# Two gated linear-attention mixers of a 1024-wide block: decay levels gathered into runs on four row groups, index scores side by side, gate by softplus, latent norms behind the products

## The reference, cut to what matters

```python
h = rmsnorm(x, g);  parts = split(h @ w_in)           # w_in: 1024 x 6744
o_mla  = causal attention; q = (rmsnorm(cq)*g) @ w_q_up, k,v = (rmsnorm(ckv)*g) @ w_kv_up
o_conv = cb * conv3(cc * cx)
rel = relu(iq . ik * 32**-0.5)                        # 8 index heads of 32
score = sum over heads of w * rel; top 64 keys of each token
o_dsa  = attention over the selected keys
a   = log_sigmoid(glr @ w_gate_up + b) / 16           # one number a key channel and token
cum = cumsum(a) inside chunks of 64 tokens
o_gla  = (q*exp(cum)) @ state  +  sum_j [q_i . (k_j * exp(cum_i - cum_j))] v_j   # j <= i in the chunk
state  = exp(last) * state + (k * exp(last - cum))^T v
merged = sum over the 4 branches of sigmoid(gate_n) * (o_n @ w_branch_n);  x = x + merged @ w_out
```

## Time and profile before

| what | value |
|---|---|
| median of 3 runs | 1791.27 us (1790.5 to 1792.84) |
| the profiled execution, its own time | 1794.49 us |
| its span in the trace | 1792.3 us |
| mean granted TensorE clock | 0.998 |
| busy: TensorE, VectorE, ScalarE, GpSimd | 99%, 71%, 53%, 2% of the span |
| HBM read | 306.57 MB, 172 GB/s over the span |
| first large mixer | about 936 to 1170 us |

### The profile page before, as it was taken

How to read it: one execution, slowest core, us unless ns; L and a number is a source line. 1 busy time by engine, 2 the same in 40 slices (tenths; PEclk the granted TensorE clock), 3 DMA queues, 4 the chain that set the end, 5 groups by cost and what they waited for, 6 DMA issues and landing times.

```text
span 1792.3 us, 24908 instructions
## 1 busy us (share of the span) xinstructions
PE 1775.2 (99%) x9702; PEld 1511.4 (84%) x9702; DVE 1271.8 (71%) x1933; ACT 948.2 (53%) x1346; POOL 30.2 (2%) x39
## 2 busy tenths in 40 slices
PE   9999999999999999999999999999999999999998
PEld 8888878888888888788888788888888878888887
DVE  7774795776577657777656977777756778677774
ACT  6554655555455546555545545455544644555553
POOL 0000000000000001000000000000000000000000
PEclk9999999999999999999999999999999999999999
DMA  8666523666566555366655534556655443456653
GB/s 272 191 179 201 176 71 96 197 183 194 175 200 184 194 176 182 107 198 189 193 183 180 179 118 130 180 182 188 190 191 171 141 156 129 152 184 194 190 195 108
DMA packets 227678, 309.25 MB, mean 173 GB/s; under 512 B 22558, under 2 KB 176318, under 8 KB 227562
## 3 DMA queue, kind: packets, MB, share of 16 engines
q1 hardware_dynamic: 227398, 307.35, 55.0%
q10 hardware_dynamic: 164, 0.30, 0.0%
HBM read 306.57 MB, written 1.05 MB: 172 GB/s over the span
## 4 chain that ended last, share of the span: by engine, by line
PE 90%; DVE 6%; ACT 2%; issue 1%; SPq 0%; DMA 0%; POOL 0%; POOLq 0%; ACTq 0%; DVEq 0%
PE ps L645 26%; PE ps L596 15%; PE ps L598 15%; PE ps L597 14%; PE ps L647 13%; DVE wlo L1733 2%; PE ps L1141 1%; PE ps L608 1%; PE ps L816 1%; DVE ev_acc L1742 1%; PE ps L842 1%; ACT whi L1239 1%; PE ps L829 1%; PE ps L784 0%; DVE m_scr L1742 0%
## 5 line engine op out<-in xcount | busy, mean ns | idle before, releaser
L1733 DVE TENSOR_TENSOR wlo<-staging,whi 128x1024 fp32r<-128x1024 f32 (+1 forms) x580 | 692.9, 1211 | 336.7 <-ACT whi L1239 336.3
L1239 ACT ACTIVATE whi<-staging 128x1024 fp32r<-128x1024 f32 (+1 forms) x580 | 606.3, 1050 | 476.9 <-PE ps L598 293.1
L645 PE MATMUL ps<-hT,whi 128*128 128x512 f32 x1984 | 624.0, 396 | 0.6 <-DVE wlo L1733 0.6
L647 PEld LDWEIGHTS ps<-hT,wlo 128*128 128x128 f32 x1984 | 372.7, 188 | 88.0
L647 PE MATMUL ps<-hT,wlo 128*128 128x256 f32 x1984 | 389.8, 278 | 0.0
L645 PEld LDWEIGHTS ps<-hT,whi 128*128 128x128 f32 x1984 | 302.0, 189 | 0.8 <-DVE wlo L1733 0.8
L596 PE MATMUL ps<-whi,fh 128*128 128x512 f32 x504 | 196.1, 389 | 0.0
L597 PE MATMUL ps<-wlo,fh 128*128 128x512 f32 x504 | 196.1, 389 | 0.0
L598 PE MATMUL ps<-whi,fl 128*128 128x512 f32 x504 | 196.1, 389 | 0.0
L596 PE MATMUL ps<-whi,hT 128*128 128x512 f32 (+3 forms) x464 | 184.7, 398 | 0.8 <-DVE wlo L1733 0.6
L598 PE MATMUL ps<-whi,hT 128*128 128x512 f32 (+3 forms) x464 | 177.4, 382 | 0.0
(11 more groups left out here) (349 smaller groups left out, 1913.2 us busy)
## 6 DMA issues: line engine op xcount, KB each, us to landing
staging<-in_w_in SPq DMA_DIRECT2D x92, 512.0 KB, 3.4
staging<-in_ffn_w_gate SPq DMA_DIRECT2D x84, 512.0 KB, 4.4
staging<-in_ffn_w_up SPq DMA_DIRECT2D x84, 512.0 KB, 4.5
staging<-in_ffn_w_down SPq DMA_DIRECT2D x84, 512.0 KB, 4.1
staging<-in_w_ffn_gate SPq DMA_DIRECT2D x44, 512.0 KB, 4.4
staging<-in_w_ffn_up SPq DMA_DIRECT2D x44, 512.0 KB, 4.6
staging<-in_w_ffn_down SPq DMA_DIRECT2D x44, 512.0 KB, 4.2
staging<-in_od_w_in SPq DMA_DIRECT2D x16, 512.0 KB, 4.3
```

The lines of the kernel that those rows point to most:

```text
L645: e.matmul(o, wh[:, kk, j * 128:j * 128 + 128], hT[:, k, :], start=k == 0, stop=False)
L647: m = e.matmul(o[:, 0:256], wl[:, kk, j * 128:j * 128 + 128], hTh[:, k, :], start=False, stop=k == KD - 1)
L1239: e.activation(high(u)[:, 0:n], stage[u % NS][:, 0:n], ACT.Copy).then_inc(*K.inc("hi", ("hi", u)))
L1733: e.tensor_tensor(low_of(u)[:, 0:n], stage[u % NS][:, 0:n], high(u)[:, 0:n].bitcast(F32), ALU.subtract).then_inc(*K.inc("lo", ("lo", u)))
```

## The change

1. *Levels.* Levels 0 to 3 run together, then 4 to 6. Each (level, head) is on its own row group of 32; the two chunks of a token tile are two column groups of 64, so only the diagonal 64x64 blocks are computed (masks 64 wide). A run takes four banks, one a head. Level runs are in rounds 25 and 30, `go` in 34, the GLA transposes in 42. Four pairs of buffers for scaled k and q instead of two.
2. *Selections* go into a buffer `near` (64 wide) by `gathered`, and ScalarE copies `near` into the padded `gat` in its round 32; its copy of `go` is in its round 33. VectorE's selections are in its rounds 25 (level 0), 27, 28, 29, 30 and 31 (levels 5 and 6).
3. *Index scores:* four row groups at a time, one group of 8 matmuls a token tile in place of two of 4.
4. *State products:* chunks 0, 1, 2 in one round, two banks, on alternating halves of the rows.
5. *Gate:* bias and log-sigmoid are one ScalarE `Softplus` with negated scale and bias; the factor -1/16 moves into the later exponentials. `glT` and `gup` have all 128 rows, the added ones zero (GpSimd memset, and SyncE waits for it before the parameter load).
6. *Latent norms:* VectorE no longer scales `nat` ahead of the `cq` transposes; the factor goes into the copies of `qn` (ScalarE) and `kn` (ScalarE, VectorE).
7. GpSimd clears `near` once; some VectorE steps of the GLA output are joined.

```diff
+    def take_two(self, one, two):
+        at = {b: n for n, b in enumerate(self.free)}
+        beside = [(b, b + 1) for b in at if b + 1 in at]
+        pair = min(beside, key=lambda p: max(at[p[0]], at[p[1]])) if beside else tuple(self.free[0:2])
...
 # TensorE, index scores
-                        for h0 in (0, 2):
-                            ps = room_pair((P, "idx", t, h0), (P, "idx", t, h0 + 1))
-                            for j in range(2):
-                                for x in range(2):
+                        ps = [b for h0 in (0, 2) for b in room_two((P, "idx", t, h0), (P, "idx", t, h0 + 1))]
+                        for j in range(2):
+                            for x in range(4):
...
 # TensorE, gla
-                    for c in range(3):
-                        t, p0 = c // 2, 64 * (c % 2)
-                        ps = room((P, "st", c))
-                        e.matmul(ps[:, 0:256], m.kd[p0:p0 + 64, t, :], N(936, 1192, t)[p0:p0 + 64, :], ...)
-                        yield
-                    for lev in range(7):
...
+                    ps = [room((P, "st", x)) for x in range(2)]
+                    for c in range(3):
+                        t, x = c // 2, c % 2
+                        w = e.matmul(ps[x][:, 256 * t:256 * t + 256], m.kd[64 * x:64 * x + 64, t, :],
+                                     N(936, 1192, t)[64 * x:64 * x + 64, :], start=True, stop=True)
...
+                    for some in (range(0, 4), range(4, 7)):
+                        for _ in range(7 if some[0] == 0 else 5):
+                            yield
+                        ps = [b for h in (0, 2) for b in room_two((P, "lev", some[0], h), (P, "lev", some[0], h + 1))]
+                        e.wait_ge(*K.at(P, "ql", some[-1]))
+                        for lev in some:
+                            kk, qq = (m.gk, m.gq) if lev == 0 else (m.kl[lev % 4], m.ql[lev % 4])
+                            for t in range(2):
+                                c = 128 * (lev % 4) + 64 * t
+                                for h in range(4):
+                                    for half in range(2):
+                                        sl = slice(t * 128 + 64 * half, t * 128 + 64 * half + 64)
+                                        w = e.matmul(ps[h][64 * half:64 * half + 64, c:c + 64],
+                                                     kk[32 * h:32 * h + 32, sl], qq[32 * h:32 * h + 32, sl], ...)
+                        for h in range(4):
+                            done(P, "lev", some[0], h)
+                    for _ in range(3):
+                        yield
+                    yield
                     for t in range(2):
                         ps = room((P, "go", t))
-                            e.wait_ge(*K.at(P, "gat", 6, 1))
+                            e.wait_ge(*K.at(P, "gat"))
...
 # ScalarE, gla
+                    e.activation(m.e1[:, :], bk(P, "gup")[:, 0:256], ACT.Softplus, scale=-1.0, bias=m.gbg[:, 0:1])
...
+                    for r, part in enumerate((top, low)):
+                        e.wait_ge(*K.at(P, "near", 6, 2))
+                        e.activation(m.gat[part, :, :, 64 * r:64 * r + 64], m.near[part], ACT.Copy)
+                    yield
                     for t in range(2):
                         e.wait_ge(*K.at(P, "go mm", t))
...
 # VectorE, gla
+                    def gathered(lev):
+                        first = lev - lev % 4
+                        c = 128 * (lev % 4)
+                        e.wait_ge(*K.at(P, "lev mm", first))
+                        for h in (0, 2):
+                            ...
+                                if lev in (3, 6):
+                                    steps += [("ev", (P, "lev", first, h + n * i + x)) for x in range(n)]
+                                e.copy_predicated(m.near[:, :, h + n * i:h + n * i + n, :], mask, ps[:, :, c:c + 128])
...
+                        if lev == 5:
+                            gathered(2)
+                        if lev == 6:
+                            gathered(4)
                         yield
                         if lev < 6:
                             scaled(lev + 1)
+                        if lev >= 3:
+                            gathered((0, 1, 3, 5)[lev - 3])
+                        if lev == 6:
+                            gathered(6)
...
 # SyncE
+                e.wait_ge(*K.at(m.P, "gup zero"))
                 load("par_" + m.P, ...
```

More of the change, by code:

```diff
@@ L176, in take_pair @@
         return b, before
+    def take_two(self, one, two):
+        at = {b: n for n, b in enumerate(self.free)}
+        beside = [(b, b + 1) for b in at if b + 1 in at]
+        pair = min(beside, key=lambda p: max(at[p[0]], at[p[1]])) if beside else tuple(self.free[0:2])
+        before = []
+        for c, user in zip(pair, (one, two)):
+            self.free.remove(c)
+            self.of[user] = c
+            before.append(self.had.get(c))
+            self.had[c] = user
+        return pair, before
     def give(self, b):
@@ L576, in room_pair, with room_two @@
                 return PS[:, b, :], PS[:, b + 1, :]
+            def room_two(one, two_):
+                pair, before = B.take_two(one, two_)
+                for user in before:
+                    if user is not None:
+                        e.wait_ge(*K.at("ev", user))
+                return [PS[:, b, :] for b in pair]
             def done(*user):
@@ L1062, in dsa @@
                         nk = 128 * (t + 1)
-                        for h0 in (0, 2):
-                            ps = room_pair((P, "idx", t, h0), (P, "idx", t, h0 + 1))
-                            if t == 0 and h0 == 0:
-                                e.wait_ge(*K.at(P + "ik T", 0))
-                            for j in range(2):
-                                for x in range(2):
[L1069 to L1074, removed]
-                            yield
+                        ps = [b for h0 in (0, 2) for b in room_two((P, "idx", t, h0), (P, "idx", t, h0 + 1))]
+                        if t == 0:
+                            e.wait_ge(*K.at(P + "ik T", 0))
+                        for j in range(2):
+                            for x in range(4):
+                                rows = slice(32 * x, 32 * x + 32)
+                                w = e.matmul(ps[x][:, j * nk:(j + 1) * nk], m.iqT[rows, j, t * 128:t * 128 + 128],
+                                             m.ikT[rows, 0, 0:nk], start=True, stop=True)
+                        w.then_inc(*K.inc("att", (P, "idx mm", t)))
+                        for x in range(4):
+                            done(P, "idx", t, x)
+                        yield
+                        yield
                         for _ in range(5):
@@ L1115, in gla @@
                     yield
+                    ps = [room((P, "st", x)) for x in range(2)]
+                    e.wait_ge(*K.at("ev", (P, "kd")))
                     for c in range(3):
-                        t, p0 = c // 2, 64 * (c % 2)
-                        ps = room((P, "st", c))
[L1119 to L1122, removed]
@@ L1123, in gla @@
-                        done(P, "st", c)
-                        yield
-                    for lev in range(7):
-                        yield
[L1127 to L1146, removed]
@@ L1170, in mla @@
                     two_ps = [room((P, "cq", q)) for q in range(2)]
-                    e.wait_ge(*K.at(P, "c scaled"))
+                    for t in range(2):
+                        e.wait_ge(*K.at("in ev", g, X2[3][0], t))
                     for k in range(3):
@@ L2611, in mixer2 @@
                 e.memset(m.gat[:, :, :, :], 0.0).then_inc(*K.inc("pad", (P, "pads")))
+                e.wait_ge(*K.at(P, "st mm"))
+                e.wait_ge(*K.at(P, "kd mm"))
+                e.memset(m.near[:, :, :, :], 0.0).then_inc(*K.inc("pad", (P, "near zero")))
                 head_norm(P + "cq", m.r1[:, :, :], 2)
```

165 lines of the change are left out of this document (89 added, 76 removed).

## The result

The changed kernel takes 1799.18 us (median of 4 runs, 1798.06 to 1802.3), the kernel before 1792.05 (4 runs): a ratio of 1.0036, 95% interval [1.002, 1.0051]. By the medians it is slower by 7.1 us, by the ratio 6.5; 4.2 were forecast, in a range of 1776 to 1809. The profiled execution took 1802.3 us, span 1800.4, mean granted clock 0.992.

The account below looks back on a forecast made before the run. TensorE, busy 99% of the span, was taken as the bound. Per mixer, 12.8 us of waits and clock added less 10.7 of work saved gave 2.1, 4.2 for both: 1791.27 + 4.2 = 1795.5 us, range 1776 to 1809.

Parts of the forecast that it names:

- The clock's cost: Granted clock falling to 1.2 GHz around the 6.5 us idle time: 1.8 us a mixer, bounds 0 and 3.4.
- wait 1: Round 31: TensorE's gate columns wait for a level-run bank freed by VectorE's level 6 selection; 6.5 us idle a mixer.
- wait 2: Round 35: TensorE's merge waits for the conv branch, late because ScalarE stands at its go copy; 3.0 us a mixer.
- the 1760 that was named: Sign: TensorE busy under 1760 us, with the forecast idle times, gives the summed case of 1795.5 us, chance 0.55.
- Levels: TensorE's seven levels a mixer, 11.3 us, become two runs costing 4.5; saved 6.8, bounds 4.0 and 8.7.
- The two dearer prices: Level runs cost 10.4 us a mixer if matmuls start strictly in program order, 13.9 at about 62 ns issue each.
- Index scores: TensorE: two pairs of row groups become four side by side; 2.1 us saved a mixer, bounds 1.5 and 2.3.
- State products: TensorE: three groups become one run of two steps; 1.4 us saved a mixer, bounds 0.9 and 1.7.
- Gate product: TensorE: all 128 rows instead of 16, so no narrow mode; 0.4 us saved a mixer, bounds 0 to 0.4.
- Wait 3: Round 42: TensorE's attention turn waits for ScalarE, itself held until the GLA transposes; 1.5 us a mixer, bounds 0 to 2.
- "All of it is hidden, so 0": Work moved on VectorE and ScalarE stays hidden by TensorE's products: 0 us; up to 2 us gained without that cover.
- Case B: Faster side, chance 0.28: waits absent or mostly covered; 1782.9 us with wait 1 alone at full clock, 1769.9 with none.

Follow-up runs that it names:

- e1: The changed kernel with VectorE's selections of levels 5 and 6 moved from round 31 to directly behind level 4's in round 30: 1787.13 us, ratio 0.9962.
- e3: The changed kernel with the first product of round 31 made nine times instead of once, keeping TensorE at work: 1796.04 us, ratio 1.0016.
- e5: The changed kernel with the second level run's four banks counted as given back in round 31, behind the gate columns, not round 30: 1791.82 us, ratio 0.9986.
- e2: e1 with TensorE's go product in round 33 instead of 34 and the GLA transposes in 41 instead of 42: 1775.79 us, ratio 0.9893.
- e11: The kernel before with only TensorE's go product moved from round 32 to 34 and its GLA transposes one round later: 1812.31 us, ratio 1.01.
- e10: e2 with VectorE's scaling of q and k for level 6 moved ahead of the two weight splits of round 29: 1774.36 us, ratio 0.9893.
- e4: The kernel before with only the change's index scores and state products: 1793.63 us, ratio 1.0001.
- e9: e4 with every second of the eight top-8 rounds of token tile 0 left out on VectorE: one run of 1788.57 us.
- e8: e4 without two small VectorE steps of the log-sigmoid, the minimum with 0 and the subtraction: one run of 1787.18 us.

## Why the prediction was right, point by point

The sign, the range and the two large waits came out; the net is the difference of two numbers three to four times its size: 14.6 us added and 11.1 saved a mixer on average, where 12.8 and 10.7 were forecast. The forecast had only 2.1 us a mixer between slower and faster, so that the sign came out is in part luck; the errors went mostly towards slower. The clock's cost was taken too small by 1.5 us and 1.4 us of waits were not foreseen, while wait 1, wait 2 and the work saved each came out 0.3 to 0.4 us better than forecast. TensorE's busy time, 1760.8 us, is just over the 1760 that was named.

- *Levels: right in kind, the gain too small.* By the same reading as for the old level, run 1 costs (1043.24 - 1041.29) - 0.24 = 1.7 us, run 2, which starts 1.2 us ahead of the next group, about 1.3: 3.0 together, where the prediction took 4.5 and had 2.6 as its lower end. The column groups run side by side, at least in part: the 32 records of a row group in run 1 take 1.52 us with the way out (1041.50 to 1043.02), 0.048 each, under the 0.055 estimated for one column group at a time, and the first eight records start within 0.05 us. Saved 8.3 a mixer, not 6.8. The two dearer prices, 10.4 us from the order and 13.9 from the issue, are both refuted here by 224 records in 3.0 us; starts 7 ns apart in that first burst are also under the floor near 25 ns that the prediction names. Of the order rule of the Trainium skill (TensorE: Matmul & The Clock Gate, "Part 2: What happens when you issue a matmul") it is the price put on it that fails, not the rule. The prediction let each record of a row group hold up all behind it. But a matmul leaves two records (448 for 224 matmuls), and eight matmuls in a row are on eight different places of the array, four row groups times two column groups. So eight starts in a burst fit matmuls that keep the order of the program, and no run here decides it.
- *Index scores:* 16 records now take 1.15 us where 8 took 1.13, so one of each pair goes: 1.7 us, predicted 2.1. *State products* 1.5 (1.4). *Gate product* 0.4 (0.4). In all 11.9 by parts and 10.9 and 11.2 by the balance above, predicted 10.7.
- *Wait 1:* 6.1 us, predicted 6.5. e1, e3 and e5 show its three sides: what ends it, that it does not depend on what TensorE does behind the `cq` transposes, and that only the choice of the bank ties TensorE to it.
- *Wait 2:* 2.7 us, predicted 3.0; e2 removes it, e11 makes it in the kernel before.
- *Wait 3:* 1.0 + 0.4 = 1.4 us, predicted 1.5; e2 removes it too.
- *Not foreseen:* 1.0 us ahead of the second run, for the scaled q of level 6. With the levels one by one this step was due a round later; e10 takes most of it away. Another 0.4 at L1118, where TensorE now comes early.
- *Clock:* 1.8 us a mixer predicted, 3.3 on average (4.7 and 1.8). The term was sized for wait 1 alone; wait 2 had its own.
- *"All of it is hidden, so 0"* for the work taken from VectorE **failed** as a rule. e4 shows that two of the change's own savings are worth little on the kernel before (predicted 7.0 us for both mixers, measured 0.2 [-1.8, 2.2] the other way, and 1.6 won by the mixers' lengths), and e9 that they are worth 3.4 us a mixer once VectorE comes earlier. The changed kernel has no wait at the `kd` transposes, with VectorE's gate and scaling steps gone. That these steps are what pays was not shown: leaving out two of them (e8) moved the wait by 0.1 us only, and the joined multiplications ahead of the `kd` step were not tried alone. The sum was little hurt, since neither the waits that the saved work brings nor the VectorE time that pays for them was in it.

Case B was the one that the better kernel realises: without the waits the prediction gave 1769.9, e2 and e10 measured 1775.8 and 1774.4, with 2.2 and 1.6 us of small waits left a mixer.

## What to carry to other kernels

Where one engine is busy 99% of the time, count a change twice: the work it takes from that engine, and each place where the engine arrives earlier or another arrives later than today. When work is gathered into bigger runs, the buffers it holds come free later and all together, so look who takes the first of them next, and where a step is moved by a round, move its partner on the other engine too. Then read the waits first: here they named both faults, and two edits of a few lines (e2) turned 7 us lost into 19 won, 19.2 by the mixers' lengths. And where the time of a run swings by more than the effect, measure the effect between two fixed points of the trace.

## What the runs showed of the hardware that was not expected

- Matmuls of 32 rows and 64 columns on four row groups and two column groups cost about 0.012 us a record from start to start (128 in 1.52 us, 96 in 1.17), in either order of the loops.
- The same idle time does not always bring the low clock. Behind wait 2, idle 2.7 us, it fell in the first mixer of the changed kernel and not in the second, but in both of e1 and e3; in e5 it fell in the first mixer behind wait 2 and not behind the 2.0 us at L1224, in the second the other way round. When it fell behind wait 2, TensorE worked for 2.9 to 3.4 us at 1.2 GHz.
